# Unscaled x in the first two groups of each adaptive layer, the token scale applied after the product

## The reference

```
shift, scale, gate = split(silu(c) @ w_ada[l] + b_ada[l])
h = x * rsqrt(mean(x*x) + eps) * norm_g[l] * (1 + scale) + shift
z = h @ w_in[l]                      # 2048 x 6656, 13 pieces of 512 columns
x = x + gate * (concat(o_fft, o_na, o_ret, o_cv) @ w_out[l])
```

## Time and profile before

| | |
|---|---|
| median of three executions | 3079.15 us |
| the profiled execution | 3075.15 us, span 3073.3 us |
| PE busy | 3037.4 us (99%) |
| DVE busy | 1939.8 us (63%) |
| ACT busy | 1453.7 us (47%) |
| POOL busy | 1291.9 us (42%) |
| granted clock, mean | 0.997 |
| layers | layer 0 from about 2183 us, layer 1 from about 2623 us |

### The profile page before, as it was taken

One profiled execution on the slowest core, in us unless ns is written; L12 is line 12 of the kernel. 1 busy time (PEld: TensorE's weight loads), 2 busy tenths in 40 slices (PEclk: granted clock), 3 DMA queues, 4 the chain that ended last, 5 costly groups with the idle time before them and its releaser, 6 DMA issues.

```text
span 3073.3 us, 46505 instructions
## 1 busy us (share of the span) xinstructions
PE 3037.4 (99%) x18814; PEld 2687.1 (87%) x18814; DVE 1939.8 (63%) x2838; ACT 1453.7 (47%) x1892; POOL 1291.9 (42%) x643
## 2 busy tenths in 40 slices
PE   8999999999999999999999999999999999999998
PEld 7888888888999999998888888888899998899986
DVE  4777675673323456686567666555479864589764
ACT  5444444444667455544544444444444454544444
POOL 5454545445566555494555454444610004510013
PEclk9999999999999999999999999999999999999999
DMA  7888887886776555555788888787666546565454
GB/s 227 279 275 262 271 277 252 287 281 182 218 178 186 155 168 145 150 174 192 238 272 264 279 268 265 262 286 259 182 185 185 160 141 198 170 189 177 151 171 164
DMA packets 486654, 662.73 MB, mean 216 GB/s; under 512 B 67992, under 2 KB 273544, under 8 KB 486184
## 3 DMA queue, kind: packets, MB, share of 16 engines
q1 hardware_dynamic: 480952, 655.05, 67.1%
q0 software_dynamic: 4448, 2.94, 0.4%
q10 hardware_dynamic: 1040, 1.78, 0.2%
HBM read 655.47 MB, written 2.10 MB: 214 GB/s over the span
## 4 chain that ended last, share of the span: by engine, by line
PE 96%; DVE 1%; ACT 1%; POOL 1%; issue 0%; DMA 0%; ACTq 0%; DVEq 0%
PE ps L924 36%; PE ps L852 23%; PE ps L929 18%; PE ps L858 11%; PE ps L842 1%; PE ps L883 1%; PE ps L1362 1%; PE ps L1152 1%; PE ps L1133 1%; POOL narrow_split_slabs L803 1%; DVE narrow_split_slabs L1854 0%; PE ps L983 0%; PE ps L1160 0%; PE ps L1190 0%; PE ps L1182 0%
## 5 line engine op out<-in xcount | busy, mean ns | idle before, releaser
L803 POOL TENSOR_TENSOR split_slabs<-stage,split_slabs 128x1024 fp32r<-128x1024 f32 x318 | 772.7, 2431 | 1319.5 <-ACT split_slabs L1417 1319.5
L1417 ACT ACTIVATE split_slabs<-stage 128x1024 fp32r<-128x1024 f32 x592 | 626.7, 1060 | 878.7 <-PE ps L929 838.2
L924 PE MATMUL ps<-split_slabs,h_split 128*128 128x512 f32 x3312 | 824.1, 391 | 0.9 <-ACT split_slabs L1417 0.9
L1417 ACT ACTIVATE narrow_split_slabs<-stage 128x1024 fp32r<-128x1024 f32 (+1 forms) x440 | 460.0, 1051 | 632.8 <-PE ps L858 559.1
L852 PE MATMUL ps<-h_split,narrow_split_slabs 128*128 128x256 f32 x5856 | 745.1, 280 | 0.0
L924 PEld LDWEIGHTS ps<-split_slabs,h_split 128*128 128x128 f32 x3312 | 622.0, 188 | 134.2 <-issue 5.1
L852 PEld LDWEIGHTS ps<-h_split,narrow_split_slabs 128*128 128x128 f32 x5856 | 702.4, 188 | 12.9 <-issue 9.0
L1854 DVE TENSOR_TENSOR split_slabs<-stage,split_slabs 128x1024 fp32r<-128x1024 f32 x274 | 349.3, 1276 | 525.2 <-ACT split_slabs L1417 523.9
L803 POOL TENSOR_TENSOR narrow_split_slabs<-stage,narrow_split_slabs 128x1024 fp32r<-128x1024 f32 (+1 forms) x181 | 435.5, 2414 | 308.1 <-ACT narrow_split_slabs L1417 300.4
L929 PE MATMUL ps<-split_slabs,h_split 128*128 128x512 f32 x1656 | 442.9, 389 | 0.3 <-POOL split_slabs L803 0.3
L1854 DVE TENSOR_TENSOR narrow_split_slabs<-stage,narrow_split_slabs 128x1024 fp32r<-128x1024 f32 x259 | 338.3, 1308 | 159.1 <-ACT narrow_split_slabs L1417 158.2
(11 more groups left out here) (259 smaller groups left out, 2113.1 us busy)
## 6 DMA issues: line engine op xcount, KB each, us to landing
stage<-in_w_in SPq DMA_DIRECT2D x360, 512.0 KB, 3.7
stage<-in_ffn_w_gu SPq DMA_DIRECT2D x352, 512.0 KB, 4.7
U<-in_w_ada SPq DMA_DIRECT2D x192, 512.0 KB, 5.3
stage<-in_ffn_w_down SPq DMA_DIRECT2D x176, 512.0 KB, 5.2
stage<-in_w_out SPq DMA_DIRECT2D x96, 512.0 KB, 4.2
stage<-in_w_in SPq DMA_DIRECT2D x80, 128.0 KB, 2.8
stage<-in_w_branch_c SPq DMA_DIRECT2D x32, 192.0 KB, 3.3
stage<-in_cmp_w SPq DMA_DIRECT2D x8, 512.0 KB, 5.2
```

The lines of the kernel that those rows point to most:

```text
L803: nc.gpsimd.tensor_tensor(slab_part(n, 1, size(n)), stage[:, n % RING, 0:size(n)], slab_part(n, 0, size(n)).bitcast(F32), ALU.subtract).th ...
L924: mm(ps[:, 2 * pair + T, :], stationary(kk, i)[:, T * P:(T + 1) * P], w[0][:, kk, :], start=first and kk == 0 and i == 0, stop=False)
L1417: return fn(slab_part(n, 0, size(n)), stage[:, n % RING, 0:size(n)], ACT.Copy)
```

## The change

The first two groups of each layer (the convolution's input) multiply a * x, rounded and split, without token scale. Beside the 256 token columns stand two more that hold the shift, so each matmul is 258 wide and its output goes to a bank of its own for each 128 output channels. Blocks 0 to 2 of x are transposed, rounded and split before the layer begins: in layer 0 during the down product of the second FFN, by DVE and ACT; in layer 1 during the output product of layer 0, blocks 0 and 1 by DVE, block 2 by PE after slab 27. Block 3 is transposed by PE after slab 0 of the layer. Meanwhile rstd is made; a product with ones spreads it over the partitions (after group 0), and `raw_evacuate` multiplies by it and adds the shift's product.

x is still scaled into y, transposed by PE (a block behind each slab of group 1), given gain and shift by ACT and split by DVE, for groups 2 to 25; group 2 waits for the last block. y has moved in memory, POOL takes slabs 0, 1, 6, 8 and 10, DVE the others, and POOL's constants and bias DMAs come after slab 12 and after the last transposes.

In the diff below the helpers that address memory and `shift_columns` are left out: it writes the two shift columns of each chunk, high part (a copy) and low part (a subtraction), four small instructions for layer 0 in the down product and four for layer 1 in the output product.

```diff
+RAW_GROUPS = 2
+XW = S + 2
+RAW = LV - 64
+RAW_BY_POOL = (0, 1, 6, 8, 10)
+RAW_END = RAW_GROUPS * DC // KC
+MASKED = RAW_END + 4
+TURN_AT, ROUND_AT = 13, (21, 29, 30)
...
+        y = u(CY, P, TT, D)
...
+        def raw_part(l, i, m):
+            if (l, i, m) == (0, 0, DC - 1):
+                return raw_last[:, :]
+            at = m * XW + (raw_views[l][2] if i else 0)
+            return raw_views[l][0][:, at:at + XW]
+        def raw_block(l, b):
+            at = raw_views[l][2] + 4 * b * XW
+            return raw_views[l][1][:, at:at + 4 * XW].rearrange("p (c w) -> p c w", c=4)[:, :, 0:S]
+        def by_tensor(l, b):
+            return b == 3 or (l, b) == (1, 2)
+        def raw_source(l, b, c):
+            if by_tensor(l, b):
+                return raw_bank(l, b, c // 2)[:, c % 2, :]
...
-        by_vector |= {n for l in range(2) for n in range(S_LAY[l] + 2, S_LAY[l] + 4 * PIECE)}
+        by_vector |= {n for l in range(2) for n in range(S_LAY[l], S_LAY[l] + 4 * PIECE) if n - S_LAY[l] not in RAW_BY_POOL}
...
+        def raw_bank(l, b, half):
+            return ps[:, (6 if b == 3 else 4) + half, :].rearrange("p (c s) -> p c s", c=2)
+        def raw_out(l, q, c):
+            return ps[:, 2 * PAIR[G_LAY[l] + q] + c, 0:XW]
...
-                if n == S_LAY[0] + 3:
+                if n == S_LAY[0] + MASKED:
...
-                if n == S_LAY[1] + 1:
-                    pool.wait_ge(*scaled.after(4, 1, 1))
...
-                    if n == S_LAY[l] + 4:
+                    if n == S_LAY[l] + MASKED:
+                        pool.wait_ge(*turned.after(3 + l, 3))
...
+            def raw_product(l, q):
+                r, g, n = 3 + l, G_LAY[l] + q, S_LAY[l] + 4 * q
+                pe.wait_ge(evacuated, g - 1)
+                for k in range(4):
+                    if q == 0:
+                        pe.wait_ge(*h_ready.after("raw", l, k))
+                    w = [slab_part(n + k, i).rearrange("p (c w) -> p c w", c=KC) for i in range(2)]
+                    pe.wait_ge(hi_done, nth[n + k])
+                    for c in range(2):
+                        for kk in range(KC):
+                            for i in range(2):
+                                mm(raw_out(l, q, c), w[0][:, kk, c * P:(c + 1) * P], raw_part(l, i, KC * k + kk),
+                                   start=k + kk + i == 0, stop=False)
+                    pe.wait_ge(*slab_split(n + k))
+                    for c in range(2):
+                        for kk in range(KC):
+                            last = mm(raw_out(l, q, c), w[1][:, kk, c * P:(c + 1) * P], raw_part(l, 0, KC * k + kk),
+                                      start=False, stop=k == 3 and kk == KC - 1)
+                    last.then_inc(slab_done, 1)
+                    if q == 0 and k == 0:
+                        pe.wait_ge(*x_half.after(r))
+                        turn_raw(l, 3, 0)
+                        pe.wait_ge(evacuated, X_READY[r])
+                        turn_raw(l, 3, 1).then_inc(*turned.mark("raw", l, 3))
+                    if q == 1:
+                        turn_scaled(r, k)
+                if q == 0:
+                    pe.wait_ge(*vec_out.after("rdiag", l))
+                    mm(ps[:, 5, 0:S], ones, u(LNX, P, S), start=True, stop=True).then_inc(*pe_out.mark("scales", l))
+            def turn_raw(l, b, T):
+                for c in range(4):
+                    at = b * WN + c * P
+                    last = transpose(raw_bank(l, b, c // 2)[:, c % 2, T * P:(T + 1) * P], x[:, T, at:at + P])
+                return last
...
-                if r == 1:
-                    for k in range(4):
-                        high(k)
-                        low(k)
-                        if k == 1:
-                            turn_x(1, 3)
-                else:
-                    high(0)
-                    turn_scaled(r, 2)
-                    high(1)
-                    low(0)
-                    turn_scaled(r, 3)
-                    high(2)
-                    low(1)
-                    high(3)
-                    low(2)
-                    low(3)
+                for k in range(4):
+                    high(k)
+                    low(k)
+                    if k == 1:
+                        turn_x(1, 3)
...
                 if b > 1:
                     pe.wait_ge(*gained.after(r, b - 2, 1))
+                else:
+                    pe.wait_ge(*vec_out.after("rstd_b", r - 3))
                 for T in range(TT):
...
-                turn_scaled(3 + l, 0)
-                turn_scaled(3 + l, 1)
...
-                    if p == 0:
-                        first_product(g0, s0, 3 + l)
+                    if p < RAW_GROUPS:
+                        raw_product(l, p)
                     else:
+                        if p == RAW_GROUPS:
+                            pe.wait_ge(*h_ready.after(3 + l, 3))
                         product(g0 + p, s0 + 4 * p, na_head=(l, p - 11) if 10 < p <= 18 else None)
...
+                        if l == 0 and (p, q) == (OUTG - 1, 3):
+                            pe.wait_ge(evacuated, X_READY[4] - 1)
+                            turn_raw(1, 2, 0)
+                            turn_raw(1, 2, 1).then_inc(*turned.mark("raw", 1, 2))
...
+            def round_raw(l, b):
+                act.wait_ge(*(turned.after("raw", l, b) if by_tensor(l, b) else block_turned.after(3 + l, b)))
+                for c in range(4):
+                    m = 4 * b + c
+                    last = fn(raw_part(l, 0, m)[:, 0:S], raw_source(l, b, c), ACT.Identity, scale=ascale[:, l, m:m + 1])
+                    if c % 2:
+                        last.then_inc(*rounded.mark("raw", l, b, c // 2))
...
-                    if f == 0 and i >= DOWN and i % DOWN == 10:
-                        round_h(1, i // DOWN - 1, pcol("mix_norm", 0, DC))
+                    if i >= DOWN and i % DOWN == 10:
+                        if f == 0:
+                            round_h(1, i // DOWN - 1, pcol("mix_norm", 0, DC))
+                        else:
+                            round_raw(0, i // DOWN - 1)
...
-                round_upto(s0 + 1 - l)
+                round_upto(s0 + 1)
                 squares(3 + l, 3)
                 rstd_of(3 + l)
                 round_upto(s0 + 2)
+                round_raw(l, 3)
                 for b in range(4):
+                    round_upto(s0 + 7 + b)
                     gain_h(3 + l, b, ascale[:, l, :], mod[:, l, 0:16])
-                    if b == 2:
-                        round_upto(s0 + 3)
...
+                        if l == 0 and p < 3 and i == ROUND_AT[p]:
+                            round_raw(1, p)
...
+            def rest_raw(l, b):
+                for half in range(2):
+                    dve.wait_ge(*rounded.after("raw", l, b, half))
+                    for c in (2 * half, 2 * half + 1):
+                        m = 4 * b + c
+                        last = v.scalar_tensor_tensor(raw_part(l, 1, m)[:, 0:S], raw_source(l, b, c), ascale[:, l, m:m + 1],
+                                                      raw_part(l, 0, m)[:, 0:S].bitcast(F32), ALU.mult, ALU.subtract)
+                last.then_inc(*h_ready.mark("raw", l, b))
             def split_h(r, b):
+                dve.wait_ge(slab_done, S_LAY[r - 3] + 4 * RAW_GROUPS - 4 + b + 1)
...
-                for b in range(3):
+                slab_lo(s0 + 2)
+                rest_raw(l, 3)
+                slab_lo(s0 + 3)
+                for T in range(TT):
+                    last = v.tensor_scalar(u(LNX, P, TT, P)[:, T, :], ident, rstd[:, r, T:T + 1], None, ALU.mult)
+                last.then_inc(*vec_out.mark("rdiag", l))
+                scale_x(r, 0)
+                slab_lo(s0 + 4)
+                for b in range(1, 4):
                     scale_x(r, b)
-                split_h(r, 0)
-                scale_x(r, 3)
-                slab_lo(s0 + 2)
-                split_h(r, 1)
-                split_h(r, 2)
-                slab_lo(s0 + 3)
-                split_h(r, 3)
+                slab_lo(s0 + 5)
...
+                    if f == 1 and i == DOWN + 3:
+                        shift_columns(0, ((0, DC - 1), (DC - 1, DC)))
+                    if i >= DOWN and 4 <= i % DOWN < 8:
+                        turn_block(r + 1, i // DOWN - 1, i % DOWN - 4)
+                    if i >= DOWN and i % DOWN == 11:
+                        if f == 0:
+                            rest_h(1, i // DOWN - 1, pcol("mix_norm", 0, DC))
+                        else:
+                            rest_raw(0, i // DOWN - 1)
...
+                def raw_evacuate(q):
+                    dve.wait_ge(slab_done, s0 + 4 * q + 4)
+                    if q == 0:
+                        dve.wait_ge(*pe_out.after("scales", l))
+                        chained(v.tensor_copy(rstd_b[:, :], ps[:, 5, 0:S]), "rstd_b", l)
+                        dve.wait_ge(*vec_out.after("pad", l))
```

(44 more changed lines are left out.)

42 lines of the change are left out of this document (28 added, 14 removed).

## The result

The changed kernel takes 3083.2 us (median of 20 executions, 3081.14 to 3089.16) against 3077.15 us for the kernel before (20 executions, 3071.78 to 3081.73): ratio 1.0023, 95% interval 1.0017 to 1.0029. It is slower by 0.23%, some 6 us. The predicted 3080.3 us and the range 3071 to 3088 stood against this, and the outcome lies in the range, in its upper part. The prediction counted from 3079.15 us for the kernel before, so as a change it was +1.1 us, against +6. The profiled execution took 3081.45 us, with a span of 3079.6 us, 6.3 us over that of before.

The account below looks back on a forecast made before the run. PE was taken as the bound, busy 3037.4 of 3073.3 us. Layer 0's start at -0.3 and layer 1's at +1.4 made +1.1 us on the median 3079.15: 3080.3 us, range 3071 to 3088.

Parts of the forecast that it names:

- within 0.2%: Whole kernel: total differs from the kernel before by no more than a measurement can tell, about 6.2 us; chance 0.57.
- the side that had 0.28: Whole kernel: total slower than the kernel before by more than about 0.2%, 6.2 us; chance 0.28.
- No gap before group 0, no wait in it.: Start of each layer: PE goes into raw_product without a gap over 0.3 us; slabs 2 and 3 arrive in time.
- Raw transposes, ones product, 258 columns.: PE work added at layer starts: transposes 0.88 us (1.76 in layer 1), ones product 0.43, two columns 0.2, dropped.
- The wait before group 2, 4.9 us in both layers.: PE waits for block 3's split h, its casts held by POOL's slab 10 subtraction: 4.9 us, bounds 3.9 and 4.9.
- Layer 0's stretch, 32.4 us.: Layer 0, last matmul before it to first of group 2: 32.4 us against 32.67, a change of -0.3.
- The wait for the token scales in layer 1, 3.5 us.: Layer 1, group 1: block 0's scaled transposes wait for DVE's copy of rstd_b, 3.5 us, bounds 0 and 5.
- a scaling that starts while POOL subtracts waits for it: Layer 1, group 1: POOL's slab 6 subtraction delays DVE's six scalings, ending them at +16.4 us instead of +13.9.
- Hidden additions: Down product and layer 0's output product: DVE and ACT's added block work costs PE nothing; 32 transposes, 14 us over 16 slabs.
- Rival 1, the clock.: Wait before group 2: clock falls to half in both layers, 3.4 us lost in each, total 3087.1 us; chance 0.23.
- Cadence.: Steady-state matmuls: 118 ns in layer 0, 113.3 in layer 1; 2.83 and 2.72 us a slab, seemingly set by the last interruption.
- rival 2: Waits at low ends give 3074.8 us; layer 0's groups 2 to 9 at 2.72 a slab give 3071.4; chance 0.15.

Follow-up runs that it names:

- the block-wise kernel: Changed kernel, but group 2 of each layer waits for the split h block by block instead of for block 3 at its start: 3071.49 us, ratio 0.9981.
- the fourth experiment: Changed kernel, but DVE instead of POOL makes slab 10's rest, behind block 3's split: 3082.36 us, ratio 1.0016.
- the sixth experiment: Changed kernel, but POOL makes slab 5's rest instead of slab 6's, which DVE makes after the first raw evacuation: 3086.61 us, ratio 1.0027.
- the last kernel: Changed kernel with block-by-block waits in group 2 and, in layer 0's output product, raw block 0's rests behind slab 27: 3067.05 us, ratio 0.9962.

## Why the prediction was right, and where it was not

The total fell in the range, but the odds did not lean to the outcome: "within 0.2%" had 0.57, and 0.23% (0.17 to 0.29) is on its edge, by the median on the side that had 0.28. Step by step:

- *No gap before group 0, no wait in it.* Right. PE goes from 2183.93 into raw_product, and stands nowhere before group 2.
- *Raw transposes, ones product, 258 columns.* Right: with no idle time left (the block-wise kernel) layer 0's stretch is 27.58 us, and 0.88 + 0.43 + 3.52 + 8 x 2.83 is 27.5. In the sum, not in each term: the raw slabs took 2.86 to 3.08 us, not 2.83, and the transposes and the ones product less than booked. The two columns cost 0.17 us a layer, where 0.2 had been reckoned and dropped. Eight of layer 1's sixteen raw transposes I booked at its start; they lie in the output product before it.
- *The wait before group 2, 4.9 us in both layers.* Right in kind, place and cause, and 0.2 to 0.3 us too long. The choice of the upper end by the nearest row held: the fourth experiment takes POOL's subtraction away, and the wait falls to 3.88.
- *Layer 0's stretch, 32.4 us.* It took 32.46.
- *The wait for the token scales in layer 1, 3.5 us.* Wrong; 0.12 us of it came. With it went 3.5 of the forecast 35.9 us, and 0.9 more for the transposes that lie elsewhere; that 32.90 was measured and not 31.3 is mostly the raw slabs: one of layer 1 took 2.90 us (2634.46 to 2637.36), not 2.72, and one of layer 0 2.86 (2190.41 to 2193.27), so the two cadences of the layers, by which I summed, do not carry over to the raw product. The times were nearly right: the six scalings ran from +11.8 to +14.2 us (foreseen 11.4 to 13.9), slab 6 was rounded at +13.6 (foreseen 12.9). What failed is the step "a scaling that starts while POOL subtracts waits for it" as used here. DVE was in the middle of its scalings (the sixth starts at 2641.75) when POOL came at 2641.65, and this time it is POOL that stands, through that scaling and slab 5's subtraction behind it:

```profile
2639.76 2.46 DVE L1931 TENSOR_SCALAR U<-x_res,rstd 128x512 f32<-128x512 f32 x6
...
2640.51 1.06 ACT L1491 ACTIVATE narrow_split_slabs<-stage 128x1024 fp32r<-128x1024 f32 x1 [1.83 <-PE ps L937]
...
2641.65 3.96 POOL L846 TENSOR_TENSOR narrow_split_slabs<-stage,narrow_split_slabs 128x1024 fp32r<-128x1024 f32 x1 [10.02 <-ACT narrow_split_slabs L1491]
2642.14 1.22 DVE L1971 TENSOR_TENSOR narrow_split_slabs<-stage,narrow_split_slabs 128x1024 fp32r<-128x1024 f32 x1
...
2643.42 0.36 DVE L2365 COPY rstd_b<-ps 128x256 f32<-128x256 f32 x1
```

  The copy ended at 2643.78 and PE began its transposes at 2643.83, after 0.12 us of waiting: there was no slack, and where POOL came 1.01 us ahead of the scalings instead of 1.89 behind their start (the sixth experiment) PE waited 1.12. The Trainium skill, "SBUF — State Buffer", section "SBUF: two separate sides", says that whichever starts first, a GpSimd instruction or a DVE one that takes the shared pair, has the pair for its whole instruction, and the other blocks. The rows agree for the single instruction; I had used half of that rule. They don't tell who has the next turn when both wait: POOL came in the midst of scalings in the kernel before as well, and there the sixth was held, just as the prediction took it. So the step went by one row that this order of work did not repeat (POOL takes 3.96 to 4.04 us for slab 6 of layer 1 in the profiles of all changed kernels but that of slab 5), and why the turn falls so is open. Two sums in this step were off as well, without effect: PE's arrivals add up to +15.5 and +14.9 us, not 15.3 and 14.8, and DVE's list in layer 0 to +14.0, not 14.6 (measured +13.8).
- *Hidden additions: "a slab's rest has some three slabs to arrive".* This is the step that failed most, 3.04 of the 4.2 us lost in the output product. It weighs how much work DVE has, not what stands behind a waiting instruction. The rests of raw block 0 cost 1.68 us, but they can start only when ACT, in its own list, has passed slab 25, and that is late for slab 23. I had asked this of every instruction at the starts of the layers and not of the ones in the cover.
- *Rival 1, the clock.* It holds in both layers, at 3.0 and 2.6 us instead of 3.4 (10.9 us a group against 13.9 and 13.5), since the clock fell late in the wait and for 6.8 us, not 10.2. It had 0.23, and by the profiles since was the likeliest thing to happen: of the ten waits of 3.8 us or more before group 2 in five profiles of this study (the changed kernel and those that keep the wait), every one was followed by half clock. The rule of the Trainium skill that the prediction weighed against the trace, "TensorE: Matmul & The Clock Gate", section "Why this matters for your kernels", that long idle gaps between bursts of matmuls let the clock drop to half, was the better guide than layer 0's single gap of 3.44 us. It isn't all of it: half clock also came after 1.94 us.
- *Cadence.* Both kinds came, in both directions, in kernels that differ nowhere near: 11.31 and 10.88 us a group. The expected luck of rival 2 in layer 0 was had, and hides 3.4 us of the loss in this profile.

So the number came out near by luck: two errors of about 3 us, a wait that did not come and one that I did not see, cancelled, the clock made the rest, and the kernel before measured 2 us less in twenty executions (3077.15) than in the three that the prediction counted from, so the number lies 2 us nearer than the change does. By the forecast's own terms: +1.1, less 3.5 (no wait in layer 1) and 0.5 (both waits before group 2 shorter), plus 1.3 (8 slabs at 2.88 instead of 2.72), plus 3.3 (the output product's 4.2 without the 0.88 already booked) and 5.6 (the clock), gives +7.3 ahead of the later groups' cadences, and the runs say +6 us. What the idea itself is worth, without the new waits, is shown by the last kernel: the two starts shrink from 67.2 us to 55.6, and the total by 11 to 12.

Left open: groups 10 to 24 take 0.2 to 0.8 us more in all changed kernels (196.4 or 196.8 against 196.0 and 196.2). The single groups differ by 0.2 to 0.4 us up and down, as the cadences do, but no run isolates it.

## What to carry to other kernels

Moving work out of the way of the first product pays only as far as nothing has to be complete at once further on: wait block by block, where the last block is due, and a chain of 4.7 us costs nothing. Before calling an addition hidden, look at the engine's list and ask what stands behind each new wait, and which other engine's list releases it; an idle engine is no cover if it is idle in a wait. For a port that two engines share, compute who starts first, and price both outcomes where they come close; a difference of 2 us in one start moved the stall from one engine to the other, and one order that looked the same gave both.

## What the runs showed of the hardware

- The clock's fall does not follow from a gap's length alone. Half clock came after waits of 1.94, 3.04, 3.05, 3.88, 4.21 and 4.6 to 4.8 us, none after others of 2.06, 3.04 and 3.44 us, one and the same wait of 3.04 us among both. It lasted 3.4 to 10.2 us, and where it lasted 6.8 behind a wait for the split h, group 2 took 2.6 to 3.0 us more than 10.88. With no wait before group 2 (two kernels, both layers) it never came there.
- Matmuls of 258 and of 256 columns differ by about 0.9 ns (0.33 us over 384).
- A POOL subtraction of 2.4 us holds two casts for 1.3 us (2.03 and 2.10 instead of 0.76), six scalings for 2.1 (4.60 instead of 2.46) and a subtraction of 1.22 us for 1.9 (3.14); beside scalings that came first it took 3.78 and 3.96 us itself. Where it came in the midst of scalings, it got in at once in the kernel before and only behind them in the changed kernels; no run here shows what decides that.
